# Expert rows of a decoder step: scattered to slots as they are made, loaded contiguously, with zeros from ScalarE's queue and an eight-operation inverse root

## The reference, cut to what matters

```python
def layer(x, ...):                       # 1024 prompt rows and 8 x 8 sample rows, D = 1024
    h = rmsnorm(x, norm1_g); proj = h @ w_in
    u, v = gelu(proj[:, :512]), layernorm(gelu(proj[:, 512:1024]), a_norm_g, a_norm_b)
    ya = u * (tril(W_s) @ v + b)         # within chunks of 128 rows, 4 heads
    yb = (trailing mean of p - p) @ b_w * b_scale
    x = x + concat(ya, yb) @ w_out
    h2 = rmsnorm(x, norm2_g)
    eidx, gates = hier_route(h2, ...)    # 1 of 4 groups, then 2 of its 8 experts
    x = x + moe_ffn(h2, eidx, gates, w1, w3, w2)   # 32 experts, silu(x@w1)*(x@w3)@w2, d_expert 512
y = rmsnorm(x, normf_g)
```

## Time and profile before

| | us |
|---|---|
| median of 3 runs | 1053.75 |
| lowest, highest | 1053.15, 1054.67 |
| the profiled execution | 1055.32 |
| its span | 1053.6 |
| TensorE busy in the span | 967.1 (92%) |
| VectorE, ScalarE, GpSimd busy | 263.9, 113.9, 149.8 |

### The profile page before, as it was taken

How to read it: one execution, slowest core, us unless ns; L and a number is a source line. 1 busy time by engine, 2 the same in 40 slices (tenths; PEclk the granted TensorE clock), 3 DMA queues, 4 the chain that set the end, 5 groups by cost and what they waited for, 6 DMA issues and landing times. The chain is left out here.

```text
span 1053.6 us, 24687 instructions
## 1 busy us (share of the span) xinstructions
PE 967.1 (92%) x10520; PEld 648.8 (62%) x10520; DVE 263.9 (25%) x848; ACT 113.9 (11%) x172; POOL 149.8 (14%) x227
## 2 busy tenths in 40 slices
PE   5999999999999942999999999999999999999940
PEld 2545545545455622868778686776868778687730
DVE  1445464553553662000101001010010100001006
ACT  0211110110111110000010100101001010010103
POOL 1000000000000012112122121211212122121100
PEclk9999999999999965999999999999999999999985
DMA  9660000000000193999999999999999999999527
GB/s 347 229 268 28 14 40 0 40 40 0 40 28 15 53 394 52 327 371 378 366 380 364 377 371 359 382 356 381 364 380 378 366 379 365 374 375 365 179 66 300
DMA packets 60793, 260.52 MB, mean 247 GB/s; under 512 B 13653, under 2 KB 14733, under 8 KB 43732
## 3 DMA queue, kind: packets, MB, share of 16 engines
q1 hardware_dynamic: 51996, 238.57, 59.0%
q0 software_dynamic: 8768, 21.54, 9.2%
HBM read 236.66 MB, written 27.21 MB: 250 GB/s over the span
## 5 line engine op out<-in xcount | busy, mean ns | idle before, releaser
L1104 PEld LDWEIGHTS ps<-hT,big 128*64 128x64 f32 x8192 | 341.1, 138 | 25.8 <-issue 24.3
L1104 PE MATMUL ps<-hT,big 128*64 128x96 f32 x8192 | 347.2, 247 | 1.0 <-DVE hT L895 1.0
L1120 PE MATMUL ps<-big,poolT 128*96 128x512 f32 x512 | 225.1, 592 | 0.8 <-issue 0.8
L1001 PE MATMUL ps<-big,hT 128*128 128x512 f32 x384 | 169.3, 600 | 3.1 <-DMA big<-in_w_in 1.7
L1120 PEld LDWEIGHTS ps<-big,poolT 128*96 128x96 f32 x512 | 81.8, 165 | 120.2 <-issue 120.2
L903 DVE TENSOR_TENSOR poolT<-u,ps 128x384 f32<-128x384 f32 x32 | 17.7, 554 | 529.0 <-PE ps L1104 529.0
L1001 PEld LDWEIGHTS ps<-big,hT 128*128 128x128 f32 x384 | 73.0, 192 | 94.0 <-issue 88.9
L505 POOL DMA_INDIRECT x_rows<-xn,sidx x32 | 46.2, 1442 | 434.3 <-ACT xn L647 434.3
L647 ACT ACTIVATE xn<-ps,gslot 96x1024 f32<-96x1024 f32 x32 | 35.5, 1110 | 409.8 <-PE ps L1120 409.8
L485 POOL DMA_INDIRECT slot_table<-ids,dest x18 | 18.4, 1022 | 325.8 <-DVE dest L762 272.9
L1058 PE MATMUL ps<-big,yT 128*128 128x512 f32 x128 | 56.4, 593 | 0.9 <-DVE yT L825 0.9
(11 more groups left out here) (151 smaller groups left out, 476.5 us busy)
## 6 DMA issues: line engine op xcount, KB each, us to landing
big<-in_exp_w SPq DMA_DIRECT2D x192, 1024.0 KB, 13.5
big<-in_w_in SPq DMA_DIRECT2D x4, 1536.0 KB, 13.2
big<-in_w_out SPq DMA_DIRECT2D x2, 2048.0 KB, 14.7
x_rows<-xres SPq DMA_DIRECT2D x8, 512.0 KB
h_rows<-xn SPq DMA_DIRECT2D x8, 512.0 KB, 2.6
big<-x_rows SPq DMA_DIRECT2D x8, 512.0 KB, 6.9
out_y_prompt<-big SPq DMA_DIRECT2D x8, 512.0 KB, 2.8
xres<-in_x_prompt SPq DMA_DIRECT2D x1, 3072.0 KB, 11.3
```

The lines of the kernel that those rows point to most:

```text
L1001: last = pe.matmul(ps[0:m, bank, :], hT[:, k, 0:m], win[:, k, part * AW:(part + 1) * AW], start=(k == 0), stop=(k == KD - 1))
L1104: last = pe.matmul(out[c * w:(c + 1) * w, j, :], up_weights(n)[:, k, j * P + c * w:j * P + (c + 1) * w], xT[:, 4 * half + k, 0:CAP], start ...
L1120: last = pe.matmul(ps[0:CAP, 5 + cols, :], hhT[:, 2 * half + k, 0:CAP], down_weights(n)[:, k, cols * 512:(cols + 1) * 512], start=(half + ...
```

## The change

1. **Rows go to their slots.** A new memory tensor `slot_rows` has a row of 4 KB for every slot. For tiles 0 to 7 GpSimd loads the stored tile back from `h2_rows` into `xg[j % 2]`, and then scatters its rows twice (once for each expert choice) to `slot_rows`. The last tile is scattered straight from its own buffer, `xn2`. The 8-byte scatters to `slot_table` stand behind the row scatters of each tile.
2. **Rows are loaded contiguously.** `fetch` and its gather are gone. ScalarE issues `load_rows(b, s)`: the first 96 slots of expert b, one plain DMA of 384 KB. The first two wait for `slots_stored`, all 18 row scatters.
3. **Zeros from ScalarE's queue.** Slots that no row fills must be finite, so in `step(1)` ScalarE issues one DMA that writes zeros from `xg[1]` to the first 96 slots of all 32 experts: 96 x 32 x 4 KB = 12.6 MB. GpSimd waits for it before its first row scatter. `xg[0]` is no longer cleared.
4. **SyncE's order.** `tabs` becomes one DMA, which waits also for both first row loads (`rows_in`); then the gate values; weight chunks 6 to 9 come after these.
5. **VectorE's order.** The plan's 17 operations stand behind the first `take_xgT`.
6. **Roots.** The shift is folded into the first guess, each Newton step is two operations for one column and three for several, and the left-over factor (`NEWTON`) is multiplied in where the root is used. One column: 8 operations for 12. Several: 11 for 15.
7. **The last stage** works in three groups of three tiles, not 5 and 4; `gf` is scaled by `NEWTON` once, ahead of it.

```diff
+        slot_rows = nc.dram_tensor("slot_rows", [NE * REG, D], F32, kind="Internal").ap()
@@ SyncE
-            sp.wait_ge(out_b, NT)
-            for n in range(CH, 10):
-                load_chunk(1, n)
             tv = slot_table.rearrange("(e r) c -> r e c", r=REG)
             sp.wait_ge(table_stored, 16 * 2 * NT)
-            for part, es in enumerate((slice(0, 2), slice(2, NE))):
-                sp.dma_start(tabs[0:CAP, es, :], tv[0:CAP, es, :]).then_inc(tabs_in[part], 16)
+            for s in range(2):
+                sp.wait_ge(rows_in[s], 16)
+            sp.dma_start(tabs[0:CAP, :, :], tv[0:CAP, :, :]).then_inc(tabs_in, 16)
...
+            sp.wait_ge(out_b, NT)
+            for n in range(CH, 10):
+                load_chunk(1, n)
@@ GpSimd
+            pool.wait_ge(trash_zeroed, 16)
+            pool.wait_ge(slots_zeroed, 16)
             for j in range(NT):
                 m = P if j < LAST else NS
+                rows, ready = (xg[j % 2], (rows_staged, 16 * (j + 1))) if j < LAST else (xn2, (x2n_ready, NT))
+                if j < LAST:
+                    pool.wait_ge(h2_stored, 16 * (j + 1))
+                    if j >= 2:
+                        pool.wait_ge(slots_stored, 16 * 2 * (j - 1))
+                    pool.dma_start(rows[0:m, :], h2_rows[P * j:P * j + m, :]).then_inc(rows_staged, 16)
                 pool.wait_ge(dest_ready, j + 1)
+                for c in range(2):
+                    pool.wait_ge(*ready)
+                    pool.indirect_dma_start(
+                        slot_rows, bass.IndirectOffsetOnAxis(ap=dest[0:m, j, c:c + 1], axis=0),
+                        rows[0:m, :], None, bounds_check=NE * REG - 1, oob_is_err=False)\
+                        .then_inc(slots_stored, 16)
                 for c in range(2):
                     pool.indirect_dma_start(
                         slot_table, ...
-            def fetch(b, s):
...
@@ ScalarE
             def step(i, cur, prev, pprev, nxt):
+                if isinstance(i, int) and i == 1:
+                    act.wait_ge(filled, 2)
+                    act.dma_start(slot_rows.rearrange("(e r) d -> r e d", r=REG)[0:CAP, :, :],
+                                  xg[1][0:CAP, :].unsqueeze(1).to_broadcast([CAP, NE, D])).then_inc(slots_zeroed, 16)
...
+            def load_rows(b, s):
+                act.dma_start(xg[s][0:CAP, :], slot_rows[bass.ds(b * REG, CAP), :]).then_inc(rows_in[s], 16)
-            def block_pair(h):
+            def block_pair(h, last=False):
                 for s in range(2):
                     b = 2 * h + s
+                    if not last:
+                        act.wait_ge(xgT_done, b + 1)
+                        load_rows(b + 2, s)
                     act.wait_ge(used, CH * b + 2)
...
+            act.wait_ge(slots_stored, 16 * 2 * NT)
+            act.wait_ge(trash_zeroed, 16)
+            for s in range(2):
+                load_rows(s, s)
@@ VectorE, rstd
-                         lambda: dve.tensor_scalar(t.bitcast(I32), a.bitcast(I32), 1, None,
-                                                   ALU.arith_shift_right),
-                         lambda: dve.tensor_scalar(y.bitcast(I32), t.bitcast(I32), -1.0, float(0x5f3759df),
+                         lambda: dve.tensor_scalar(y.bitcast(I32), a.bitcast(I32), -0.5, float(0x5f3759df),
                                                    ALU.mult, ALU.add)]
-                for _ in range(3):
+                for three in (3.0, 12.0, 768.0):
...
-                    chain += [lambda: dve.tensor_scalar(t, t, -0.5, 1.5, ALU.mult, ALU.add),
-                              lambda: dve.tensor_tensor(y, y, t, ALU.mult)]
+                    chain.append(lambda three=three: dve.scalar_tensor_tensor(y, t, three, y, ALU.subtract, ALU.mult))
@@ VectorE, last stage
-            for turn, tiles in enumerate((range(0, 5), range(5, NT))):
+            dve.tensor_scalar(gf[:, :], gf[:, :], NEWTON, None, ALU.mult).then_inc(ssf_set, 1)
+            for turn, tiles in enumerate((range(0, 3), range(3, 6), range(6, NT))):
                 norm_tiles(turn, tiles)
```

More of the change, by code:

```diff
@@ L39 @@
 EPS = 1e-6
+NEWTON = -1.0 / (2 * 4 * 1024)
 BIG = 1.0e30
@@ L151, in build @@
         tabs = sb("tabs", [P, NE, 2], I32)
-        gidx = [sb(f"gidx{s}", [P, 1], I32) for s in range(2)]
         sidx = [sb(f"sidx{s}", [P, 1], I32) for s in range(2)]
@@ L184, in build @@
         trash_zeroed = sem("trash_zeroed")
+        slots_zeroed = sem("slots_zeroed")
+        slots_stored = sem("slots_stored")
+        rows_staged = sem("rows_staged")
         x2_stored = sem("x2_stored")
@@ L242, in build @@
         plan_ready = sem("plan_ready")
-        tabs_in = [sem(f"tabs_in{n}") for n in range(2)]
+        tabs_in = sem("tabs_in")
         chunk_in = [sem(f"chunk_in{c}") for c in range(2 * CH)]
         used = sem("used")
-        gidx_ready = sem("gidx_ready")
         sidx_ready = sem("sidx_ready")
@@ L519, in block_pair @@
                     b = 2 * h + s
[L520 to L523, removed]
                     if not_first(h):
@@ L538, in block_pair @@
                     scatter_add(ys[s][0:CAP, :], sidx[s][0:CAP, :], rows_out[s])
-            pool.wait_ge(tabs_in[0], 16)
-            for s in range(2):
-                fetch(s, s)
-            pool.wait_ge(tabs_in[1], 16)
-            pool.wait_ge(trash_zeroed, 16)
+            pool.wait_ge(tabs_in, 16)
+            pool.wait_ge(gates_stored, 32)
             pool.wait_ge(x2_stored, 16 * NT)
@@ L648, in block_pair @@
                                    scale=gslot[s][0:CAP, 0:1]).then_inc(y_ready, 1)
+            act.wait_ge(slots_stored, 16 * 2 * NT)
+            act.wait_ge(trash_zeroed, 16)
+            for s in range(2):
+                load_rows(s, s)
             block_pair(0)
-            with act.Fori(1, NE // 2) as h:
+            with act.Fori(1, NE // 2 - 1) as h:
                 block_pair(h)
+            block_pair(NE // 2 - 1, last=True)
             over = act.value_load(plan[0:1, 2 * MAXO:2 * MAXO + 1], min_val=0, max_val=MAXO)
@@ L783, in step @@
                     reached(dve, h2_stored, 16 * (i - 1))
-                    dve.tensor_scalar(xn2[0:m, :], xres[0:m, i - 1, :], ss2[0:m, 1:2], None, ALU.mult)\
+                    dve.tensor_scalar(xn2[0:m, :], xres[0:m, i - 1, :], ss2[0:m, 1:2], NEWTON, ALU.mult, ALU.mult)\
                         .then_inc(x2n_ready, 1)
@@ L860, in _, with take_xgT, block_pair @@
                  ], gate_step, 0, gate_step)
+            def take_xgT(b):
+                dve.wait_ge(xgT_done, b + 1)
+                dve.tensor_tensor(xT[:, :, 0:CAP], wide[:, :, 0:CAP], g2t[:, :].unsqueeze(2).to_broadcast([P, KD, CAP]),
+                                  ALU.mult).then_inc(xgT_ready, 1)
+            def block_pair(h, last=False):
+                for s in range(2):
+                    b = 2 * h + s
+                    dve.wait_ge(silu_done, b + 1)
+                    dve.wait_ge(used, CH * b + 4)
+                    dve.tensor_tensor(hhT[:, :, 0:CAP], s1T, up3, ALU.mult).then_inc(hhT_ready, 1)
+                    if not (last and s):
+                        take_xgT(b + 1)
+            take_xgT(0)
             own, end, one = blk[:, 0, :], blk[:, 1, :], blk[:, 2, :]
@@ L890, in _ @@
                  lambda: dve.tensor_copy(plan[:, :], planf[:, :])], plan_step, 0, plan_ready)
-            def take_xgT(b):
-                dve.wait_ge(xgT_done, b + 1)
-                dve.tensor_tensor(xT[:, :, 0:CAP], wide[:, :, 0:CAP], g2t[:, :].unsqueeze(2).to_broadcast([P, KD, CAP]),
-                                  ALU.mult).then_inc(xgT_ready, 1)
-            def block_pair(h, last=False):
-                for s in range(2):
-                    b = 2 * h + s
-                    dve.wait_ge(silu_done, b + 1)
-                    dve.wait_ge(used, CH * b + 4)
-                    dve.tensor_tensor(hhT[:, :, 0:CAP], s1T, up3, ALU.mult).then_inc(hhT_ready, 1)
-                    if not (last and s):
-                        take_xgT(b + 1)
-            take_xgT(0)
             block_pair(0)
```

31 lines of the change are left out of this document (16 added, 15 removed).

## The result

The changed kernel takes **1081.3 us** (median of 4 runs, 1077.4 to 1084.5) beside 1054.0 for the kernel before on the same chip: ratio 1.026, 95% interval 1.0232 to 1.0288, slower by 27 us. The forecast was 1045.0, 8.8 us faster. In the profiled executions (1077.35 and 1055.32) the spans are 1075.7 and 1053.6: 22.1 us more.

The account below looks back on a forecast made before the run. TensorE, busy in 92% of the span, was taken as the bound, so only its idle time and stages without it could give much. Hand-over -9.5, zeros +2.7, last stage -2.0: -8.8 from 1053.75 gives 1045.0 us, range 1041.0 to 1052.5.

Parts of the forecast that it names:

- Hand-over: Between the last tile and the first expert: row scatters and plain row loads replace the gather, -9.5 us (bounds -13.5 to -5.8).
- Last stage: End of the kernel: three groups let VectorE start behind the third square, -2.0 us (bounds -2.3 to -1.3).
- Roots: Roots in the tiles: worth nothing beside full tiles; in the sample tile four fewer operations bring `dest_ready` 0.65 us sooner.
- Steady experts: Experts in steady running: ScalarE's added DMA issue per load and GpSimd's missing gather cost 0.
- Zeros: Early tiles: the zeros delay the load of tiles 2 to 8 to 71.0 us, so TensorE stalls +2.7 us.
- the small late loads: Start of tile 1: they land at 56.1 us, needed by 55.9; 0.2 us at worst, inside the 2.7.
- Even sharing: Early tiles: zeros and tile load share the DMA engines evenly, adding 8.5 us to the load, landing at 71.0.
- Rival 2: Early tiles: slow zeros, perhaps from row pitch, make the tile load late; 1055.6 to 1072.6 us; chance 0.15.
- clock term: In rival 2, early tiles: a long TensorE stall also lowers the granted clock, +2.1 us.
- gate values and `tabs`: First expert: both are off the path and end before 426 us, when ScalarE needs the gate gather; cost 0.
- rival 1: Hand-over: row scatters as slow as the slow gathers, 9.1 us for 5.4, +3.7, giving 1048.7 us; chance 0.17.
- Rivals 1 and 3: Rival 3, second expert: weights come late behind slow small writes, TensorE waits up to 4 us, 1049 us; chance 0.08.

## Why the prediction was wrong

**Hand-over: right.** Forecast -9.5, measured -10.6 when both kernels are counted from the last residual addition. The second row scatter landed after 3.5 us, not 5.4; the first load took 4.55 from its issue, not 3.8; `dest_ready` came 0.64 sooner (0.65).

**Last stage: right.** -2.0 forecast, -2.3 in the trace of the changed kernel and in the kernel with this edit alone. Roots: eight operations and 1.7 us, as said.

**Steady experts: right.** 587.15 us from the second expert to the last stage in both kernels; ScalarE's issues and the missing gather cost nothing.

**Zeros: wrong, and most of the miss.** Against the profiled execution the forecast is 30.9 us too low (+22.1 for -8.8), and the tiles have 25.9 of these (+28.6 for +2.7). The step that failed is the sentence on the small late loads, "at the edge, 0.2 at worst and inside the 2.7". It took the cost of saturated queues for one small transfer, 5.3 us, and added it to the last landing. But of the small loads SyncE had nine still to issue when its issues became slow. Each took about 1.8 us more (2.4 for 0.6), so SyncE was through with them 14 us later (63.9 for 49.7), and then the last one landed 11 us after its issue, in place of about 1. The sum is 24 us, of which 5 were slack: that is the stop of 19.2 us. Second, the tile load is behind these on SyncE's queue, so it was issued 14 us late before any sharing began. "Even sharing" of the engines, the term I worked out, wanted 21 us from issue to landing; it came near with zeros from 128 partitions (54.99 to 77.87, 22.9 us), but in the changed kernel the load took 31.4 (63.94 to 95.34), 10 more than forecast, although its queue had the larger share of the engines from 80 to 90 us. Why is not shown. Third, 403 GB/s for the zeros was read from a load to 128 partitions and put on a write from 96, which ran at 294. The run with 128 partitions shows what the number 96 is worth: 1059.9 for 1081.3 us. It is 10 us above the late zeros (1049.5); 3.5 of these are the stop for the small late loads, whose issues still take 1.1 to 1.5 us, and 3.5 more the stop for v.

**Rival 2** had the right sign, the right place and a wrong mechanism. It decided from a tile load that lands at 77.7 and gave 1055.6 to 1072.6; the load landed at 95.3, near its far end, but most of the time was lost before, at the small loads, and the reason was not the pitch; the zeros' packets were slower, but 1.4 times (223 for 164 ns) and not twice. Its clock term was right in kind: about 4 us went to matmuls after the stop.

**A cover that failed: gate values and `tabs`,** costed at 0. They were off the path to the first expert, but stood ahead of chunks 6 to 9, and beside them the transfers crawled: +6.4 us in the first expert, the second part of the miss. With late zeros and 128 pieces 0.7 of it is left (24.0 us for 23.3). The evidence was in the earlier trace rows: a gather of 9.1 us behind 1088 small writes, a lone one 3.8. The prediction calls that gather the first and the slowest; it was the second, and the first took 10.1. I used it for rival 1, as a danger to scatters that the new order takes out of the way, and did not ask what else would now stand behind the small writes. It also hid a gain: the kernel before paid the same 5 us.

Rivals 1 and 3 did not occur: the last row scatter was not slow (3.5 us), and TensorE never waited for weights after the first expert.

What stays open: how a transfer from 96 partitions makes another queue's *issue* slow (the runs show that it does, 2.4 us against 1.1 to 1.6), why the tile load then needed 31.4 us, and what exactly ended the stop in the first expert.

## What to carry to other kernels

Cost a large background transfer by what its issuing blocks on other queues, not only by the share of bandwidth: count the small DMAs that are still to be issued after it and look at who waits for the last of them. Give bulk writes to memory all 128 partitions, even at the price of more bytes as here, and start them when nothing small is pending; moving one `dma_start` by 40 us was worth 32 us here. And look for transfers of many 8-byte pieces: one layout with longer pieces was worth 5 us in either kernel, without any new mechanism.

## What the runs showed that I had not expected

- Beside 12.6 MB written from 96 partitions, a DMA issue of SyncE takes 2.3 to 3.1 us in place of 0.46 to 0.67, whether ScalarE or GpSimd issued the large one. Beside 12.6 or 16.8 MB from 128 partitions it is 1.1 to 1.6 us; with two transfers of 1 MB in flight 1.07 in the mean beside writes and 0.6 beside loads.
- From 50 to 60 us the writes from 96 partitions leave the DMA engines busy all the time and the core at 293 to 303 GB/s (319 as eight DMAs); from 128 it is 386 to 401.
- Behind gate values written as 1088 pieces of 8 bytes the weights move at 69 GB/s from 410 to 415 us, where it is 416 when the same values go as 128 pieces; a gather of rows beside them takes 10.1 us for 4.1.
- An indirect scatter of 64 rows of 4 KB lands 3.5 us after its start, one of 8-byte entries after 2.1.
